# Rounding weight chunks in two halves around the exponentials: a hybrid two-layer encoder on one Trainium2 core

## The reference, cut to what matters

```
proj = x @ w_in                                  # both mixers
s = q @ k.T * d**-0.5 (+ c_t - c_s in FoX), masked
p = softmax(s)                                   # differential: p = p1 - lam * p2
o = p @ v;  h = concat(norm(o) ...) @ w_out
x = LN(alpha * x + h);  x = LN(alpha * x + (silu(x @ w1a) * (x @ w1b)) @ w2)
```

## Time and profile before

| | us |
|---|---|
| runs of the kernel before | 1375.19, 1378.5, 1379.66 (median 1378.5) |
| the profiled execution | 1378.56 |
| its span | 1376.8 |
| TensorE busy in the span | 1342.0 (97%) |
| GpSimd, ScalarE, VectorE busy | 532.0, 492.4, 475.2 |
| the differential attention | about 184 to 272 |
| the forgetting attention with its projections | about 680 to 973 |

### The profile page before, as it was taken

The page is one execution under the profiler, slowest core; times in us unless marked ns, Lnnn a source line. Parts: engine busy times, 40 slices in busy tenths (PEclk is TensorE's granted clock), DMA queues, the critical chain, the costliest instruction groups (busy, mean ns, idle before and its releaser), DMA issues.

```text
span 1376.8 us, 18931 instructions
## 1 busy us (share of the span) xinstructions
PE 1342.0 (97%) x7304; PEld 1119.5 (81%) x7304; DVE 475.2 (35%) x927; ACT 492.4 (36%) x817; POOL 532.0 (39%) x421
## 2 busy tenths in 40 slices
PE   7999999999999999999999999999999999999997
PEld 6888877779888888888888888777798888888886
DVE  4375547482111111011644565554641111110105
ACT  3413166433222322211365565654232223222111
POOL 4523232224444444643234222323145444445440
PEclk9999999999999999999999999999999999999999
DMA  6311031123333332333124212212233333323221
GB/s 207 122 62 62 32 123 62 32 60 94 92 99 110 97 92 77 123 104 97 62 62 126 62 32 63 62 62 72 82 92 92 95 109 101 93 77 122 100 99 61
DMA packets 141416, 119.60 MB, mean 87 GB/s; under 512 B 5680, under 2 KB 120592, under 8 KB 141328
## 3 DMA queue, kind: packets, MB, share of 16 engines
q1 hardware_dynamic: 141088, 118.10, 27.6%
q10 hardware_dynamic: 240, 0.31, 0.1%
HBM read 116.20 MB, written 2.10 MB: 86 GB/s over the span
## 4 chain that ended last, share of the span: by engine, by line
PE 89%; DVE 5%; ACT 3%; issue 2%; DMA 1%; POOL 0%; SPq 0%; ACTq 0%; DVEq 0%; POOLq 0%
PE banks L526 27%; PE banks L528 26%; PE banks L527 26%; PE banks L896 2%; PE banks L1054 1%; PE banks L1019 1%; PE banks L1035 1%; ACT w_hi L1207 1%; PE banks L598 1%; PE banks L914 1%; PE banks L969 1%; PE banks L956 1%; DMA x_res<-in_x_dram 1%; PE banks L1027 0%; DVE x_res L1763 0%
## 5 line engine op out<-in xcount | busy, mean ns | idle before, releaser
L1165 POOL TENSOR_TENSOR w_lo<-w_raw,w_hi 128x512 fp32r<-128x512 f32 x417 | 531.8, 1305 | 813.3 <-ACT w_hi L1207 715.6
L526 PE MATMUL banks<-xT_lo,w_hi 128*128 128x512 f32 (+2 forms) x1024 | 384.7, 376 | 3.4 <-issue 2.1
L528 PE MATMUL banks<-xT_hi,w_hi 128*128 128x512 f32 (+2 forms) x1024 | 380.7, 372 | 0.0
L527 PE MATMUL banks<-xT_hi,w_lo 128*128 128x512 f32 (+2 forms) x1024 | 380.7, 372 | 0.0
L1207 ACT ACTIVATE w_hi<-w_raw 128x2048 fp32r<-128x2048 f32 (+2 forms) x106 | 198.1, 1869 | 170.9 <-PE banks L528 143.4
L526 PEld LDWEIGHTS banks<-xT_lo,w_hi 128*128 128x128 f32 (+1 forms) x1024 | 192.4, 188 | 38.8 <-issue 6.5
L528 PEld LDWEIGHTS banks<-xT_hi,w_hi 128*128 128x128 f32 (+1 forms) x1024 | 192.2, 188 | 33.7
L527 PEld LDWEIGHTS banks<-xT_hi,w_lo 128*128 128x128 f32 (+1 forms) x1024 | 192.5, 188 | 32.6
L1820 DVE TENSOR_TENSOR banks<-silu_g,banks 128x512 f32<-128x512 f32 x44 | 30.6, 696 | 405.8 <-PE banks L528 405.8
L526 PE MATMUL banks<-w_lo,xT_hi 128*128 128x256 f32 (+1 forms) x480 | 158.8, 331 | 2.5 <-issue 1.8
L528 PE MATMUL banks<-w_hi,xT_hi 128*128 128x256 f32 (+1 forms) x480 | 153.7, 320 | 0.0
(11 more groups left out here) (193 smaller groups left out, 1248.9 us busy)
## 6 DMA issues: line engine op xcount, KB each, us to landing
w_raw<-in_ffn_w_dram SPq DMA_DIRECT2D x92, 512.0 KB, 4.7
w_raw<-in_ffn_w_dram SPq DMA_DIRECT2D x20, 1024.0 KB, 4.9
w_raw<-in_fox_w_in_dram SPq DMA_DIRECT2D x16, 1024.0 KB, 5.9
w_raw<-in_even_w_in_dram SPq DMA_DIRECT2D x13, 1024.0 KB, 4.9
w_raw<-in_even_w_out_dram SPq DMA_DIRECT2D x4, 1024.0 KB, 5.0
w_raw<-in_fox_w_out_dram SPq DMA_DIRECT2D x4, 1024.0 KB, 4.9
x_res<-in_x_dram SPq DMA_DIRECT2D x4, 512.0 KB, 7.5
out_dram<-x_res SPq DMA_DIRECT2D x3, 512.0 KB, 2.6
```

The costliest lines, as they stand in the source:

```text
L526: mm(acc, l_hi, r_lo, start=first, stop=False)
L527: mm(acc, l_lo, r_hi, start=False, stop=False)
L528: return mm(acc, l_hi, r_hi, start=False, stop=final)
L1165: ins = nc.gpsimd.tensor_tensor(w_lo[c % RING][:, a:a + n], w_raw[c % RAW][:, a:a + n], w_hi[c % RING][:, a:a + n].bitcast(F32), ALU.subtract)
```

## The change

`hi_upto` is replaced by two calls at the rounding places of both attentions. `hi_left` first rounds all that is due before chunk c, then the left half of c (1024 columns), and signals nothing to others. `hi_right` rounds the right half and raises `hi_ready`. In the differential attention the right half follows the exponentials of the next step and stands ahead of that step's copy to `pT_diff`; in FoX it stands behind the exponentials of the same entry, ahead of its `pT_fox`. GpSimd's condition stays the whole chunk.

```diff
+            def hi_left(c):
+
+                hi_upto(c)
+                if rounded[0] > c:
+                    return
+                act.wait_ge(w_loaded[c % RAW], need[c])
+                act.wait_ge(*chunk_used[c - RING])
+                n = chunks[c][2] // 2
+                step(fn(w_hi[c % RING][:, 0:n], w_raw[c % RAW][:, 0:n], ACT.Copy))
+
+            def hi_right(c):
+
+                if rounded[0] > c:
+                    return
+                n = chunks[c][2] // 2
+                chain(fn(w_hi[c % RING][:, n:2 * n], w_raw[c % RAW][:, n:2 * n], ACT.Copy), hi_ready)
+                rounded[0] += 1
+
@@ differential attention, ScalarE, step s: behind the exponentials, ahead of pT_diff
+                if s - 1 in DIFF_ROUND:
+                    hi_right(DIFF_ROUND[s - 1])
...
                 if s in DIFF_ROUND:
-                    hi_upto(DIFF_ROUND[s] + 1)
+                    hi_left(DIFF_ROUND[s])
@@ FoX, ScalarE, entry i
                 if i in round_at:
-                    hi_upto(round_at[i] + 1)
+                    hi_left(round_at[i])
...
+                if i in round_at:
+                    hi_right(round_at[i])
                 if s is not None and 2 <= s < F_UNITS + 2:
                     prob_copy(s - 2)
```

## The result

| | before | after |
|---|---|---|
| median of 9 runs each, same chip, us | 1375.82 | 1381.69 |
| lowest and highest | 1371.79, 1379.87 | 1380.79, 1386.25 |
| ratio of the times, with its 95% interval | | 1.0043 (1.0029 to 1.0058) |
| profiled execution, its span | 1378.56, 1376.8 | 1386.25, 1384.3 |
| mean granted clock in the span | 0.995 | 0.991 |

The change makes the kernel 5.9 us slower. The forecast was 1385.0, 6.4 us above the kernel before as three runs had it (1378.5); the nine runs put that kernel at 1375.82, so the forecast step fits better than the forecast time, which is 3.3 us too high.

A forecast was written before the change was run, and what follows sets the result against it. TensorE was taken as the bound, busy 1342.0 of 1376.8 us, so only its waits count. The terms 0.7 + 2.9 + 1.7 - 0.3 + 0.8 + 0.6 = 6.4 us, on 1378.5, gave 1385.0 us; range 1380 to 1389.

The forecast's parts named there:

- the rivals at 1383.3 and 1381.4: 1383.3: clock stays up behind the new stall, chance 0.15; 1381.4: GpSimd's pieces do not meet VectorE's small instructions, 0.17.
- Step 18: End of differential attention: right half ahead of Ln costs 1.1, GpSimd's pieces meeting VectorE's root refinement 1.8; +2.9 us.
- Step 12: Differential attention, TensorE's longest stall, up to 246.69: the copy to pT_diff begins later, +0.7 us (bounds 0 and +1.06).
- The other steps of the differential attention: Steps 1, 4 and 8: the wait at 200.40 goes, later copies cost little or nothing; -0.3 us in all.
- FoX: Second attention: only entries with their own exponentials matter much; two terms, +0.8 and +0.6 us, the rest 0.
- step 3: FoX entry with its own exponentials: the right half pushes pT_fox, TensorE waits until 759.3; +0.8 us.
- step 11: FoX entry with its own exponentials: pT_fox is pushed where a wait of 0.38 us exists already; +0.6 us.
- The entries with roots alone: FoX entries with roots: roots 0.9 us earlier, what follows 0.2 to 0.4 later; 0, with 0.8 either way.
- The clock: One more slow period behind the new idle time at 272.5: 3.4 us at half speed, +1.7 us (bounds 0 and 3.4).
- the rival of a period twice as long: The slow clock lasts twice as long at the new stall: 1386.7 us, chance 0.10.
- The rival that weights would be late: Later hi_ready at split chunks makes TensorE wait 1 us at three or four chunks: 1388 to 1389 us, chance 0.07.
- The rival of a faster kernel: Six roundings in the chain of waits each give back up to 0.86 us: 1373.4 us, chance 0.04.

The follow-up runs named there:

- gate18: The changed kernel with GpSimd's first two pieces of the chunk out0 3 held until the first o_ready; 1379.19 us, ratio 1.0021 to the kernel before.
- again: The changed kernel timed once more, unaltered; 1380.96 us, ratio 1.0037 to the kernel before.
- only18: The kernel before with only the chunk of step 18 rounded in two halves; 1380.24 us, ratio 1.0026 to the kernel before.
- whole18: The changed kernel with the chunk of step 18 rounded whole again, ahead of the last junk; 1377.55 us, ratio 1.0008 to the kernel before.
- late18: The changed kernel with step 18's right half behind the roots' Ln and Exp instead of ahead; 1379.40 us, ratio 1.0032 to the kernel before.
- pick: The kernel before with step 12's rounding moved whole to step 14, halves only at step 1 and in FoX entries without own exponentials; 1372.83 us, ratio 0.9984.
- pick2: The same kernel as pick, timed once more; 1374.42 us, ratio 0.9984 to the kernel before.

## Why the prediction was right, point by point

The step of 6.4 us was right, the time of 1385.0 was 3.3 us too high with its base. 1381.69 is by itself nearer to the rivals at 1383.3 and 1381.4 (whose terms add up to 2.9, not the 2.8 written); that the meeting did come is seen in the trace and in gate18, not in the time. The prediction's reading of TensorE's waits left out the largest row, on the load of x (7.9 us), and one on spans (2.2); both are the same after the change.

**Step 18** was forecast as 1.1 for the half and 1.8 for the meeting: 2.9. It is 1.0 and 1.5, 2.56 in all. The order of events was as written. GpSimd's two pieces run from 273.51 to 276.01; the first small instruction ends with the first of them (274.82), the second with the other (276.04), the third runs free, and no L1706 meets a piece. Only the size was off: the forecast let the second end 2.9 us behind the pieces' start, and it was 2.53.

**Step 12** was forecast at +0.7 and is +0.18. The step that failed reads "But the next instruction, junk, needs the products of L956, which end at 243.01; of the 0.86 us half is lost there". The timeline of ScalarE, then of TensorE, after the change:

```profile
244.45 0.37 ACT L1318 ACTIVATE junk<-banks,stats 128x128 f32<-128x128 f32 x1
...
246.88 1.06 ACT L1215 ACTIVATE w_hi<-w_raw 128x1024 fp32r<-128x1024 f32 x1
247.97 0.60 ACT L1360 ACTIVATE pT_diff<-banks 128x512 f32<-128x512 f32 x1
...
240.84 0.61 PE L956 MATMUL banks<-bv,pT_diff 128*128 128x128 f32 x4
...
244.01 0.83 PE L956 MATMUL banks<-bv,pT_diff 128*128 128x128 f32 x6
...
248.72 0.44 PE L979 MATMUL banks<-ident,p_map 128*128 128x128 f32 x1 [2.80 <-ACT pT_diff L1360]
```

junk starts at 244.45, right behind the left half and without a wait, while the L956 that the prediction means still runs, from 244.01 to 244.84. It isn't the one that this junk needs. In step s ScalarE squares the unit s - 4 (L1300), and TensorE multiplies the unit s - 3 (L956 in `diff_values(s - 3)`): the junk of step 13 reads the unit of TensorE's step 12, the row that ends at 241.45, before the left half begins (243.36). The kernel before has it alike: that L956 ends at 239.61, the rounding begins at 241.52. So nothing of the 0.86 us was lost, and the copy is late by 1.06 - 0.86 = 0.2 us: it starts at 247.97, where 245.95 plus the shift of 1.84 there is 247.79. The lower bound of the forecast, "0 (junk not held up, and half a rounding gained)", should by the same numbers have been this 0.2.

**The other steps of the differential attention** were forecast at -0.3 and are -0.53: the wait at 200.40 goes, and 0.21 us appear a step earlier, as written (0.15).

**FoX** was forecast at +1.4 and comes to +0.8 by 881, and to +1.1 with the wait at 963.17, but only two of its terms stand: step 3 (0.78 for 0.8) and step 11 (0.54 for 0.6). Steps 7 and 15 were held to end "within 0.1 us of TensorE's need" and cost 0.32 and 0.33. The entries with roots alone, taken as 0 "with 0.8 either way", give back 1.15 in all. So the sum came out near the forecast because two errors partly cancel, which is luck. What they gain was seen at 749.19, where a wait of 0.60 us is gone. Roots 0.9 us earlier release GpSimd's pieces otherwise in time (736.76 to 740.55 and from 744.79 on, where before they ran from 740.84 on), and VectorE's two scalings took 1.58 us in place of 2.10:

```profile
747.40 1.58 DVE L1940 TENSOR_SCALAR p_fox<-p_fox,small 128x128 f32<-128x128 f32 x2
...
744.79 3.78 POOL L1165 TENSOR_TENSOR w_lo<-w_raw,w_hi 128x512 fp32r<-128x512 f32 x3 [4.24 <-DVE qn L1881]
```

That this is how the 0.49 us came about is read from the two traces; no run took the meeting away by itself.

**The clock** was forecast at +1.7. In four of the six profiled executions that have the new 2.5 us wait, a slow period follows it; in the two others it does not, and in none of the eight profiled ones without that wait is there one at this place. The stretch behind L598 in "again", then in only18 (clock third from the right):

```profile
272.20:275.60 3.40, 3.40 (x11) 2.87 (x12) 2.57 (x4) 0.69 (x1) 1.97 (x2) 0.54 0.02 5
```

```profile
272.60:276.00 3.40, 3.40 (x19) 2.86 (x20) 2.88 (x4) 0.69 (x1) 1.99 (x2) 1.00 0.02 5
```

Where it fell it cost 1.5 to 1.6 us (the growth of the shift behind L598: 1.59, 1.49, 1.49 and 1.59). In the changed kernel's first profile:

```profile
279.50:282.90 3.40, 3.40 (x14) 2.69 (x13) 0.82 (x1) 0.33 (x1) 1.97 (x2) 0.66 0.07 17
```

Each of the four periods lasted 3.4 us, so the rival of a period twice as long did not come. By the clock of all runs, the six kernels with the long wait lose 7.8 us to slow clock on average (62 runs) and the kernel before 5.6 (108 runs): +2.3. But whole18, gate18 and late18, which have the other split chunks and waits of at most 1.0 us at step 18, lose 6.8 (36 runs), +1.2 already. What the wait itself takes is the other 1.1 us (standard error 0.3), which agrees with 1.5 us in four of six executions. So the mechanism stands and its size was 1.1 in the mean, not 1.7; a period is an outcome of some executions. The +1.2 had no term in the forecast, and its cause stays open. That the clock as a whole came near 1.7 is luck. The Trainium skill ("TensorE: Matmul & The Clock Gate", Why this matters for your kernels) warns of longer gaps between bursts; the waits of 2.5 and 1.79 us here were followed by half speed in most traces (four of six, and eight of 14), and the traces decide.

So the sum of 6.4 was 5.0 to 5.9 as measured, from +2.6 at step 18, +0.2 at step 12, -0.5 at the early steps, +1.1 in FoX and +2.3 of clock. The largest term and its mechanism are right; that the rest sums to nearly the forecast 3.5 is in part luck. Of the signs that the prediction named, the wait on o_even came (2.52 for 2.9), the two small instructions took 1.88 us together (near 2), the waits on pT_fox were 0.91 and 0.92 (0.8 and 1.0), and the wait at step 14 was 2.80, not 3.3. One sign of being wrong came in part: the waits on pT_diff shrank in sum, by the one at 200.40 that the forecast itself let go. The rival that weights would be late did not come: the wait for low parts is 0.6 us as before. The rival of a faster kernel had a true part, the entries with roots, and pick lives on it and on the rounding moved from step 12 to 14.

## What to carry to other kernels

- Cutting a long instruction on an in-order engine makes what stands between the halves earlier, and what stands behind the second half pays for it. Look per site for the place where the engine really idles: here six sites cost 4.7 us and the others gave 1.7.
- Ask of each moved semaphore whom it sets free and beside whom that engine will then run. Half of the largest term was no instruction moved ahead of another, but GpSimd's pieces beside VectorE's.
- A term of zero "either way" should be worked out per site where there are sixteen of them; here one sum was nearly right because two errors cancelled in part.
- Which product an instruction waits for is read from the kernel (which unit it reads), not from the product whose row stands nearest in time: the 0.5 us that step 12 was forecast too high is that slip.

## What the hardware showed that was not expected

- GpSimd beside VectorE costs a small VectorE instruction 0.5 to 1.0 us (0.69, 0.88, 1.19, 1.22 us in place of 0.17 to 0.22), and the larger ones too: three products of 128 x 512 took 4.08 us in place of 2.14, with GpSimd's two pieces at 3.10 in place of 2.50. Holding the pieces back moved the cost to where TensorE waits little (0.28 us), or to a wait for the pieces themselves (1.09 us).
- The same wait of 2.5 us was followed by half speed in four executions and by full speed in two. What a wait costs through the clock comes so in a share of executions. The spread of the kernel before (1371.4 to 1379.9 us) goes with the clock: in the experiments its executions under 1373 us had a mean granted clock of 0.997 or 0.998, those over 1379 of 0.995.
- A slow period can hide a meeting. With half speed behind step 14 (pick2) the pieces of GpSimd beside VectorE cost TensorE nothing; at full speed (pick) they cost it 1.0 us ten us later, in the same kernel.
